# The adaLN modulation as column-tiled matmuls and the sums of squares run up on VectorE, in a fused block of linear attention, FFN, HGRN and Fourier mixing

## Chip, cores and metric

One core of one Trainium2 chip. The metric is the device time of one launch in microseconds (us), median of the runs. The engines are named PE (TensorE, the matrix engine), DVE (VectorE), ACT (ScalarE), POOL (GpSimd) and SP (SyncE, which here only starts DMA transfers). Everything is fp32. "Plain fp32" products appear in the trace as two LDWEIGHTS/MATMUL records each; the large linear layers use instead a split of each operand into a high part in the type fp32r and a low rest, and three products of one record each.

## What is computed

A token sequence of 512 (width 1024) goes through a hybrid layer (a gated delta rule with 4 heads beside a dilated attention with 8 heads, output projection, FFN of width 2816) and then through a second block of two layers: a gated recurrence (HGRN, 16 heads, with a context of 256 tokens) and a Fourier mixer. Two things in it matter here. Each layer of the second block scales, shifts and gates by a vector made from a conditioning vector `c` (and `c_ctx` for the context in the first layer):

```python
def rms_norm(x, g):
    var = jnp.mean(xf * xf, axis=-1, keepdims=True)
    return (xf * lax.rsqrt(var + EPS)).astype(x.dtype) * g

def adaln(cvec, w, b):
    m = jax.nn.silu(cvec) @ w + b          # (1024) @ (1024, 3072), two layers
    return jnp.split(m, 3, axis=-1)
...
        sh_l, sc_l, gt_l = adaln(c, ada_w[i], ada_b[i])
        h_lat = rms_norm(x_lat, norm_g[i]) * (1.0 + sc_l[:, None]) + sh_l[:, None]
...
        x_lat = x_lat + gt_l[:, None] * y_lat
```

And seven times the root mean square of a token's 1024 features is needed.

## The kernel before

The activations lie with features on the 128 partitions: 1024 features are KT = 8 blocks of a partition tile by 512 tokens. A linear layer is cut into units: a unit is a weight block of 1024 rows (8 blocks k) by 128 columns, 512 KB, loaded by SP (L361) into one of NST = 4 slots of `stage`, in the order of the list `units`. SP waits at each load until the slot is free (`stage_free`), and so a load that waits holds up every load behind it. ACT copies the slot to the high part `wh` (L975, `high`), DVE subtracts to the low part `wl` (L1362, `weight_low`, which frees the slot), both NSPLIT = 3 units ahead of PE. PE then runs 8 x 3 matmuls of 512 columns into one of three PSUM banks (L477 to L479). A tile is what one PSUM bank collects, one unit mostly, two units for `hg_w_out`.

**The modulation.** `ada_w` has 2 layers of 24 column blocks. Each is a further unit in the same list, not linear (`lin=False`, "raw" below). POOL (block at L414) multiplies the whole slot by the silu of the vector (L431, 128x1024), adds halves to 512 (L435) and to 256 columns (L439) in `mod`; PE sums over the partitions with two plain fp32 matmuls of one moving column (L460). The first 16 blocks of layer 0 are done for two vectors, so there are 40 such sums for layer 0 and 24 for layer 1. The 40 run during the attention and the delta rule, where PE takes them at the end of a step (`modulation(step)`, 32 steps, up to 1.3 sums a step). The other 24 stand in the FFN: two raws after each of the first two column pairs of a round, one after the later ones, until there are none left.

**The FFN.** Three rounds of 8, 8 and 6 column pairs. A pair is two `w_up` units (gate and up half); ACT evacuates each (L1183), DVE convolves (L1623, L1626), ACT applies silu (L1185), DVE multiplies (L1630), ACT and DVE split (L1187, L1632, semaphore `flo`). After the pairs the 8 tiles of `w_down` need all of them in order. In `finish_tile(t)` ACT first makes the high part of the unit three ahead and then waits for tile t, so evacuations stand behind that load in its queue.

**The norms.** After each tile n of a layer that adds to the residual, DVE adds the bank to `xT` (L1399 or L1401, `residual`), behind the low part of the weights three units ahead; ACT squares it to `sq` (L993, two buffers); PE adds over the partitions and over n with `ones` as stationary operand, a plain fp32 matmul of 512 columns (L512, `sum_mm`), 8 for each norm, placed one tile late. After the last `w_down` round there are two norms at once, of x and of x scaled by `final1`, 16 matmuls. The context norm (256 columns) runs in FFN round 2. The first norm, at the start, is not touched.

The attention stage in between has one more set of names: `g_*` are 128x512 tiles of the delta rule, `G["m.."]`, `xx`, `xt`, `tt` its doubling steps; `sm`, `pr`, `pT` are the attention's scores, probabilities and their transposes.

## Time and profile before

| | us |
|---|---|
| three runs | 2291.93, 2295.78, 2300.16 |
| median | 2295.78 |
| the profiled execution | 2289.31 |
| its span, first to last instruction | 2287.6 |
| busy in it: PE / DVE / ACT / POOL | 2125.4 / 1432.6 / 770.8 / 285.2 |
| mean granted TensorE clock | 0.964 |

The profiled execution is 6.5 us under the median and 1.7 us over its own span. Busy time is the union of an engine's instructions. The rows that later sections rest on are quoted in a section of their own; times in them are us from the start of the span unless marked ns.

### The profile page before, as it was taken

The page shows a single profiled execution, that of the slowest core. Times are in us where ns is not written, and L with a number is a line of the kernel's source. Part 1 is how long each engine was busy: PE and PEld are TensorE (multiplying, and loading weights), DVE is VectorE, ACT ScalarE, POOL GpSimd, SP SyncE. Part 2 cuts the span into 40 slices and gives each one's busy share as a digit, 9 for nine tenths or more (in the row PEclk, how much of TensorE's full clock was granted, in tenths as well). Part 3 has the DMA queues.
Part 4 walks back from the last instruction along what each step waited for, and adds up shares of the span by engine and source line. Part 5 has one row for each costly group of instructions (what it writes and reads, how often), then busy time and mean ns, then how long its engine had stood idle before and what let it go on. Part 6 is the DMA issues. An engine that isn't in the chain of part 4 may idle for free.

```text
span 2287.6 us, 27275 instructions
## 1 busy us (share of the span) xinstructions
PE 2125.4 (93%) x10891; PEld 1739.3 (76%) x10891; DVE 1432.6 (63%) x2240; ACT 770.8 (34%) x1145; POOL 285.2 (12%) x196
## 2 busy tenths in 40 slices
PE   6998778888999999799999999999999698999997
PEld 4876666656888887588888888888888586687875
DVE  5623777836847676568777887788877732433332
ACT  4363222244324433422333333323223323432222
POOL 0002677503413131000000000000000000000000
PEclk9999898888999999899999999999999799999999
DMA  4331111223434343111111111111111032132220
GB/s 143 100 85 39 45 47 47 74 89 103 140 102 138 111 118 113 55 56 48 55 56 47 56 47 56 47 56 47 47 56 54 12 109 66 39 91 83 83 83 37
DMA packets 311134, 164.58 MB, mean 72 GB/s; under 512 B 6268, under 2 KB 307938, under 8 KB 311010
## 3 DMA queue, kind: packets, MB, share of 16 engines
q1 hardware_dynamic: 311010, 162.85, 24.5%
q8 instruction: 87, 1.43, 0.3%
q14 instruction: 37, 0.30, 0.0%
HBM read 160.73 MB, written 2.10 MB: 71 GB/s over the span
## 4 chain that ended last, share of the span: by engine, by line
PE 75%; DVE 16%; issue 4%; ACT 4%; POOL 0%; SPq 0%; DMA 0%; DVEq 0%; ACTq 0%; POOLq 0%
PE bank L477 18%; PE bank L479 17%; PE bank L478 17%; PE bank L797 3%; DVE KC L1729 2%; DVE MT L1756 2%; DVE QQ L1735 2%; DVE QC L1731 2%; PE bank L512 2%; PE bank L496 1%; PE bank L495 1%; PE bank L494 1%; PE bank L913 1%; PE bank L841 1%; PE bank L822 1%
## 5 line engine op out<-in xcount | busy, mean ns | idle before, releaser
L1362 DVE TENSOR_TENSOR wl<-stage,wh 128x1024 fp32r<-128x1024 f32 (+1 forms) x248 | 310.6, 1254 | 581.7 <-ACT wh L975 581.6
L477 PE MATMUL bank<-hh,wh 128*128 128x512 f32 x1408 | 578.2, 411 | 31.8 <-DVE hl L1383 15.3
L975 ACT ACTIVATE wh<-stage 128x1024 fp32r<-128x1024 f32 (+1 forms) x248 | 260.0, 1050 | 924.3 <-PE bank L479 596.7
L479 PE MATMUL bank<-hh,wl 128*128 128x512 f32 x1408 | 553.8, 393 | 0.0
L478 PE MATMUL bank<-hl,wh 128*128 128x512 f32 x1408 | 552.6, 392 | 0.0
L477 PEld LDWEIGHTS bank<-hh,wh 128*128 128x128 f32 x1408 | 267.0, 190 | 92.7 <-issue 32.5
L479 PEld LDWEIGHTS bank<-hh,wl 128*128 128x128 f32 x1408 | 266.4, 189 | 58.3
L478 PEld LDWEIGHTS bank<-hl,wh 128*128 128x128 f32 x1408 | 267.7, 190 | 48.1 <-issue 0.7
L477 PE MATMUL bank<-gh,wh 128*128 128x512 f32 x432 | 180.0, 417 | 14.0 <-DVE gl L1888 5.1
L431 POOL TENSOR_TENSOR mprod<-stage,gs 128x1024 f32<-128x1024 f32 x64 | 131.2, 2050 | 462.3 <-DMA stage<-in_ada_w 457.5
L478 PE MATMUL bank<-gl,wh 128*128 128x512 f32 x432 | 170.3, 394 | 0.0
L479 PE MATMUL bank<-gh,wl 128*128 128x512 f32 x432 | 170.0, 394 | 0.0
L797 PEld LDWEIGHTS bank<-QC,KC 128*128 128x128 f32 x1024 | 132.1, 197 | 30.9 <-issue 27.3
L797 PE MATMUL bank<-QC,KC 128*128 128x128 f32 x1024 | 141.9, 283 | 14.4 <-DVE MT L1756 12.6
L477 PEld LDWEIGHTS bank<-gh,wh 128*128 128x128 f32 x432 | 82.4, 191 | 38.5 <-DVE gl L1888 6.5
L494 PE MATMUL bank<-ch,wh 128*128 128x256 f32 x384 | 111.0, 289 | 0.0
L495 PE MATMUL bank<-cl,wh 128*128 128x256 f32 x384 | 108.6, 283 | 0.0
L496 PE MATMUL bank<-ch,wl 128*128 128x256 f32 x384 | 108.6, 283 | 0.0
L435 POOL TENSOR_TENSOR mprod<-mprod 128x512 f32<-128x512 f32 x64 | 100.9, 1576 | 5.0
L478 PEld LDWEIGHTS bank<-gl,wh 128*128 128x128 f32 x432 | 82.5, 191 | 21.3 <-issue 4.8
L1729 DVE TENSOR_TENSOR KC<-KK,QQ 128x512 f32<-128x512 f32 x112 | 79.2, 707 | 29.0 <-PE bank L797 29.0
L479 PEld LDWEIGHTS bank<-gh,wl 128*128 128x128 f32 x432 | 82.2, 190 | 17.7
(307 smaller groups left out, 3149.0 us busy)
## 6 DMA issues: line engine op xcount, KB each, us to landing
stage<-in_hg_w_in SPq DMA_DIRECT2D x80, 512.0 KB, 3.6
stage<-in_ada_w SPq DMA_DIRECT2D x48, 512.0 KB, 3.6
stage<-in_w_up SPq DMA_DIRECT2D x44, 512.0 KB, 3.8
stage<-in_ft_w_in SPq DMA_DIRECT2D x32, 512.0 KB, 3.9
stage<-in_w_in SPq DMA_DIRECT2D x28, 512.0 KB, 3.8
stage<-in_w_down SPq DMA_DIRECT2D x16, 512.0 KB, 3.9
stage<-in_hg_w_out SPq DMA_DIRECT2D x16, 512.0 KB, 4.0
stage<-in_ft_w_out SPq DMA_DIRECT2D x16, 512.0 KB, 3.8
```

Source lines behind the costliest of these rows:

```text
L431: do(nc.gpsimd.tensor_tensor(mprod[:], stage[:, u["slot"], :, :], view(silc[:, v:v + 1], [[2, KT], [0, P]]), ALU.mult), f"stage_free{u['sl ...
L435: do(nc.gpsimd.tensor_tensor(mprod[:, 0:4, :], mprod[:, 0:4, :], mprod[:, 4:8, :], ALU.add))
L477: pe.matmul(bank[t % NLIN][:], wh[:, s, k, :], xh[:, k, :], start=a, stop=False)
L478: pe.matmul(bank[t % NLIN][:], wh[:, s, k, :], xl[:, k, :], start=False, stop=False)
L479: mm = pe.matmul(bank[t % NLIN][:], wl[:, s, k, :], xh[:, k, :], start=False, stop=b)
L494: pe.matmul(o, wh[:, s, k, :], ch[:, k, :], start=a, stop=False)
L495: pe.matmul(o, wh[:, s, k, :], cl[:, k, :], start=False, stop=False)
L496: mm = pe.matmul(o, wl[:, s, k, :], ch[:, k, :], start=False, stop=b)
L797: mm = pe.matmul(b[:, a * P:(a + 1) * P], kc[:, a * P:(a + 1) * P], qc[:, a * P:(a + 1) * P], start=True, stop=True)
L975: do(A.activation(wh[:, l % NSPLIT, 0:nk, :], stage[:, u["slot"], 0:nk, :], ACT.Copy), "hi_ready")
L1362: do(X.tensor_tensor(wl[:, l % NSPLIT, 0:nk, :], stage[:, u["slot"], 0:nk, :], wh[:, l % NSPLIT, 0:nk, :].bitcast(F32), ALU.subtract), f"s ...
L1729: do(X.tensor_tensor(view(kc[:, 0:1], flat), view(KK[:, 0, 0:1], sel), view(QQ[:, 0, 0:1], sel), ALU.mult))
```

## The change

**Modulation.** POOL does nothing any more. A raw unit is now 4 blocks of rows by 256 columns of `ada_w` (still 512 KB, in rows of 1 KB instead of 512 B), 48 of them, two (`kh` 0 and 1) to a block of 256 outputs, 12 blocks a layer. `silp` holds silu(c) and silu(c_ctx) in columns 0 and 1 of 32, the rest zero. PE itself waits for the slot and runs four plain fp32 matmuls per unit (L450 of the changed kernel): stationary `silp` 128x32, moving the 256 weight columns, the k-th one into partitions 32k to 32k+31 of bank 7, that is with the k-th column tile of the array. ACT copies the bank to `modrow` (`mod_rows`), and PE turns and adds the four partial rows with two matmuls against the 128x2 constant `pick` (`mod_columns`, L494). Layer 0 is done in 12 of the 33 attention steps, layer 1 between the two units of the first 12 FFN pairs. Both vectors are always computed. A raw's slot is now freed by PE, at PE's place in the program.

**Sums of squares.** For five of the norms (numbers m = 1, 2, 3, 5, 6), DVE adds squares 1 to 6 to their predecessors (`running`, L1446 and L1448), between the low part of the weights and the residual of the next tile, and PE runs two matmuls at the end (`sum_of`, four at the double norm) in place of eight (sixteen). ACT's square n waits for the running sum before it.

```diff
@@ -54,15 +54,14 @@
+BLOCKS = 12
+SQ_ADDS = {1: 0, 2: 6, 3: 12, 5: 24, 6: 30}
+SQ_SUMS = {1: 8, 2: 10, 3: 12, 5: 16, 6: 18}
...
@@ -112,8 +112,8 @@
-    raws = [dict(w="ada_w", layer=l, rows=(0, 8), col=j * P, lin=False, raw=l * 24 + j)
-            for l in range(2) for j in range(24)]
+    raws = [dict(w="ada_w", layer=l, rows=(4 * kh, 4), col=j * 2 * P, lin=False, raw=(l * BLOCKS + j) * 2 + kh)
+            for l in range(2) for j in range(BLOCKS) for kh in range(2)]
     late = raws[24:]
@@ -125,8 +125,9 @@
                 add("w_up", (0, 8), half * FF + j * P, "h")
-            units.extend(late[:2 if j < 2 else 1])
-            late = late[2 if j < 2 else 1:]
+                if half == 0:
+                    units.extend(late[:2])
+                    late = late[2:]
         for n in range(KT):
...
@@ -411,33 +424,6 @@
-        @block.gpsimd
...
-                        do(nc.gpsimd.tensor_tensor(mprod[:], stage[:, u["slot"], :, :], view(silc[:, v:v + 1], [[2, KT], [0, P]]),
-                                                   ALU.mult),
-                           f"stage_free{u['slot']}" if end else None, u["load"] + 1 if end else None)
-                        do(nc.gpsimd.tensor_tensor(mprod[:, 0:4, :], mprod[:, 0:4, :], mprod[:, 4:8, :], ALU.add))
-                            pool.wait_ge(S("mod_mm"), n - 1)
-                        do(nc.gpsimd.tensor_tensor(mod[:, n % 2, :, :], mprod[:, 0:2, :], mprod[:, 2:4, :], ALU.add), "mod_ready")
@@ -451,15 +437,19 @@
+                    j, kh = u["raw"] // 2, u["raw"] % 2
+                    if u["raw"] == 0:
+                        pe.wait_ge(S("silc_ready"), 2)
                     if u["raw"] == 24:
                         pe.wait_ge(S("ada0"), 1)
-                    for v in modulated(u["raw"]):
-                        n = modulation_sums(u["raw"]) + v
-                        pe.wait_ge(S("mod_ready"), n + 1)
-                        for k in range(2):
-                            mm = pe.matmul(bank[7][:, 2 * u["raw"] + v:2 * u["raw"] + v + 1], mod[:, n % 2, k, :],
-                                           ones[:, 0:1], start=(k == 0), stop=(k == 1))
-                        mm.then_inc(S("mod_mm"), 1)
+                    pe.wait_ge(S(f"stage_in{slot}"), 16 * (u["load"] + 1))
+                    if kh == 0 and j:
+                        pe.wait_ge(S("mod_ev"), j)
+                    w = raw_view(u)
+                    for k in range(4):
+                        mm = pe.matmul(bank[7][32 * k:32 * k + 32, 0:2 * P], silp[:, 4 * kh + k, :], w[:, k, :],
+                                       start=(kh == 0), stop=(kh == 1))
+                    mm.then_inc(S(f"stage_free{slot}"), 1)
                     return
@@ -496,6 +486,14 @@
+            def mod_columns(j):
+                pe.wait_ge(S("mod_ev"), j + 1)
+                for i in range(2):
+                    c = 2 * P + 2 * (2 * j + i)
+                    mm = pe.matmul(bank[7][:, c:c + 2], modrow[:, j % 2, i * P:(i + 1) * P], pick, start=True, stop=True)
+                mm.then_inc(S("mod_mm"), 1)
...
@@ -512,13 +510,14 @@
-            def residual_units(t0, sums, first_x):
-                for n in range(KT):
-                    units_to(t0 + n, first_x if n == 0 else None)
-                    if n:
-                        sums(n - 1)
-                sums(KT - 1)
+            def sum_of(m, part, width=T, b=3, buf=sq):
+                if part == 0:
+                    pe.wait_ge(S("sq_add"), SQ_ADDS[m] + (12 if m == 3 else 6))
+                else:
+                    pe.wait_ge(S("sq_ready"), KT * m + (2 * KT if m == 3 else KT))
+                pe.matmul(bank[b][:, 0:width], ones[:], buf[:, part, 0:width], start=(part == 0), stop=(part == 1)
+                          ).then_inc(S("sq_used"), 1)
@@ -612,10 +611,12 @@
-                while not units[pos[0]]["lin"] and modulation_sums(units[pos[0]]["raw"] + 1) <= 1.3 * (step + 1):
-                    unit(units[pos[0]])
-                    pos[0] += 1
+                if step - 1 in MOD_STEP:
+                    mod_columns(MOD_STEP[step - 1])
+                if step in MOD_STEP:
+                    for _ in range(2):
+                        unit(units[pos[0]])
+                        pos[0] += 1
...
@@ -743,19 +748,18 @@
                         mm.then_inc(S("cx_T"), 1)
-                        if j:
-                            sum_mm(2 * KT + j - 1, j - 1, CT)
                 if r < 2:
...
                     if r == 1:
-                        sum_mm(3 * KT - 1, KT - 1, CT)
+                        for part in range(2):
+                            sum_of(2, part, CT)
                     units_to(t1_ + KT - 1)
...
                         units_to(t1_ + n, ("flo", pairs) if n == 0 else None)
-                        for k in ([n - 1] if n else []) + ([n] if n == KT - 1 else []):
-                            sum_mm(3 * KT + 2 * k, k)
-                            sum_mm(3 * KT + 2 * k + 1, k, b=4)
+                    for part in range(2):
+                        sum_of(3, part)
+                        sum_of(3, part, b=4, buf=facc)
                 pairs += len(ROUND[r])
...
@@ -992,6 +999,19 @@
+            def square_of(m, n, src, name, value, width=T):
+                if n < 2:
+                    act.wait_ge(S("sq_used"), SQ_SUMS[m])
+                else:
+                    act.wait_ge(S("sq_add"), SQ_ADDS[m] + (2 if m == 3 else 1) * (n - 1))
+                act.wait_ge(S(name), value)
+                do(A.activation(sq[:, n % 2, 0:width], src, ACT.Square), "sq_ready")
+                if m == 3:
+                    if n == 0:
+                        act.wait_ge(S("flo"), FT)
+                    do(A.activation(facc[:, n % 2, :], src, ACT.Square, scale=vcol("final1", n)), "sq_ready")
...
@@ -1031,6 +1051,13 @@
+            def mod_rows(j):
+                u = raw_last[j]
+                act.wait_ge(S(f"stage_free{u['slot']}"), u["load"] + 1)
+                if j >= 2:
+                    act.wait_ge(S("mod_mm"), j - 1)
+                do(A.activation(modrow[:, j % 2, :], bank[7][:, 0:2 * P], ACT.Copy), "mod_ev")
...
@@ -1181,6 +1216,8 @@
                         evac(t, A.activation(fraw[:, 2 * (p % 2) + half, 2:2 + T], bank[t % NLIN][:], ACT.Copy))
+                    if p < BLOCKS:
+                        mod_rows(BLOCKS + p)
                     act.wait_ge(S("fconv"), 2 * p + 1)
...
@@ -1400,8 +1436,20 @@
+            def running(m, n, width=T):
+                if not 0 < n < KT - 1:
+                    return
+                dve.wait_ge(S("sq_ready"), KT * m + (2 * n + 2 if m == 3 else n + 1))
+                if n > 1:
+                    dve.wait_ge(S("sq_add"), SQ_ADDS[m] + (2 if m == 3 else 1) * (n - 1))
+                do(X.tensor_tensor(sq[:, n % 2, 0:width], sq[:, n % 2, 0:width], sq[:, (n - 1) % 2, 0:width], ALU.add), "sq_add")
+                if m == 3:
+                    do(X.tensor_tensor(facc[:, n % 2, :], facc[:, n % 2, :], facc[:, (n - 1) % 2, :], ALU.add), "sq_add")
...
             do(X.memset(halfeps, EPS), "const_set")
+            do(X.memset(silp[:], 0.0), "silp_zero")
             for k in range(KT):
...
@@ -1608,6 +1656,7 @@
                 weights_behind(T_OUT + n)
+                running(1, n - 1)
                 residual(T_OUT + n, n)
@@ -1631,8 +1680,12 @@
                     p += 1
+                    if r == 1:
+                        running(2, j - 1, CT)
                 for n in range(KT):
                     weights_behind(t1_ + n)
+                    if r == 2:
+                        running(3, n - 1)
                     residual(t1_ + n, n)
...
```

Order of PE's instructions in the attention stage, steps 2 and 3 of the first token block; `m_87` and `m_88` are the two level masks, L670 (L671 changed) the matmul that opens a step. Before:

```order
L588 MATMUL bank<-bqkv 128x384
L670 MATMUL bank<-g_xx,g_m_87 128x128 x4
L600 MATMUL bank<-ident,pr 128x128 x2
L680 MATMUL bank<-g_tt,g_xt 128x128 x4
L683 MATMUL bank<-g_xt,g_tt 128x128 x4
L588 MATMUL bank<-bqkv 128x512
L670 MATMUL bank<-g_xx,g_m_88 128x128 x4
L460 MATMUL bank<-ones,mod 128x1 x4
L600 MATMUL bank<-ident,pr 128x128 x3
```

and changed:

```order
L587 MATMUL bank<-bqkv 128x384
L671 MATMUL bank<-g_xx,g_m_87 128x128 x4
L450 MATMUL bank<-stage,silp 32x256 x8
L599 MATMUL bank<-ident,pr 128x128 x2
L681 MATMUL bank<-g_tt,g_xt 128x128 x4
L684 MATMUL bank<-g_xt,g_tt 128x128 x4
L587 MATMUL bank<-bqkv 128x512
L671 MATMUL bank<-g_xx,g_m_88 128x128 x4
L494 MATMUL bank<-small,modrow 128x2 x2
L599 MATMUL bank<-ident,pr 128x128 x3
```

The eight matmuls of a block stand where two small sums stood every other step, and the two that turn the rows a step later.

PE in the FFN between the two `w_up` units of a pair, where one raw stood. Before:

```order
L477 MATMUL bank<-hh,wh 128x512
L478 MATMUL bank<-hl,wh 128x512
L479 MATMUL bank<-hh,wl 128x512
L460 MATMUL bank<-ones,mod 128x1 x2
L477 MATMUL bank<-hh,wh 128x512
L478 MATMUL bank<-hl,wh 128x512
```

and changed (the L494 is that of the block before):

```order
L467 MATMUL bank<-hh,wh 128x512
L468 MATMUL bank<-hl,wh 128x512
L469 MATMUL bank<-hh,wl 128x512
L494 MATMUL bank<-small,modrow 128x2 x2
L450 MATMUL bank<-stage,silp 32x256 x8
L467 MATMUL bank<-hh,wh 128x512
L468 MATMUL bank<-hl,wh 128x512
```

The eight matmuls are now in the row of linear units, and so is PE's wait for the slot.

DVE in the tiles of `w_out` (L1362 and L1398 are the low part of the weights, L1399 and L1435 the residual). Before:

```order
L1362 TENSOR_TENSOR wl<-stage,wh 128x1024
L1399 TENSOR_TENSOR xT<-xT,bank 128x512
L1362 TENSOR_TENSOR wl<-stage,wh 128x1024
L1399 TENSOR_TENSOR xT<-xT,bank 128x512
L1362 TENSOR_TENSOR wl<-stage,wh 128x1024
L1399 TENSOR_TENSOR xT<-xT,bank 128x512
```

and changed:

```order
L1398 TENSOR_TENSOR wl<-stage,wh 128x1024
L1435 TENSOR_TENSOR xT<-xT,bank 128x512
L1398 TENSOR_TENSOR wl<-stage,wh 128x1024
L1446 TENSOR_TENSOR sq<-sq 128x512
L1435 TENSOR_TENSOR xT<-xT,bank 128x512
L1398 TENSOR_TENSOR wl<-stage,wh 128x1024
L1446 TENSOR_TENSOR sq<-sq 128x512
L1435 TENSOR_TENSOR xT<-xT,bank 128x512
```

From the third tile on an addition stands ahead of each residual.

## Rows read from the trace of the kernel before

**Rows 1.** Page of the kernel before, parts 1 and 2: busy time, granted clock

```profile
PE 2125.4 (93%) x10891; PEld 1739.3 (76%) x10891; DVE 1432.6 (63%) x2240; ACT 770.8 (34%) x1145; POOL 285.2 (12%) x196
...
PEclk9999898888999999899999999999999799999999
```

**Rows 2.** Busy time by stretch, two stretches, with its line of columns

```profile
core 0: us, PE busy (x) PEld busy (x) DVE busy (x) ACT busy (x) POOL busy (x), PEclk, DMA share, GB/s
207.00:460.00 253.00, 206.00 (x1240) 164.98 (x1240) 189.76 (x420) 62.84 (x127) 156.64 (x112) 0.88 0.17 49
552.00:625.00 73.00, 73.00 (x340) 60.85 (x339) 63.37 (x63) 27.35 (x38) 35.33 (x22) 1.00 0.46 137
```

**Rows 3.** Chain of waits by line, 207 to 460 us, shares of that stretch

```profile
by line: PE bank L609 9.2%; issue 8.1%; PE bank L683 6.2%; PE bank L670 5.8%; DVE pr L1488 5.3%; PE bank L680 4.6%; PE bank L588 4.1%; PE bank L460 3.5%; DVE g_tt L1512 2.8%; PE bank L633 2.7%; DVE pr L1493 2.5%; DVE g_ee L1525 2.5%; PE ban
```

**Rows 4.** Chain of waits by line, 230 to 245 us

```profile
by line: POOL mprod L431 15.9%; PE bank L680 11.9%; POOL mprod L435 11.5%; DVE pr L1493 11.2%; PE bank L683 10.4%; POOL mod L439 9.8%; PE bank L670 7.3%; PE bank L588 7.0%; PE bank L460 6.4%; PE bank L600 6.2%; issue 2.7%; POOLq L411 0.1%
```

**Rows 5.** Groups by line, DVE, 207 to 460 us: busy us, mean ns, idle

```profile
L1488 DVE CUSTOM_DVE_ANT_0 pr<-sm,dcnt 128x128 f32<-128x128 f32 (+3 forms) x32 | 24.9, 778 | 0.0
L1553 DVE TENSOR_TENSOR g_m<-g_lt,gmask 128x512 f32<-128x512 f32 x20 | 24.3, 1213 | 0.0
L1493 DVE TENSOR_SCALAR pr<-pr,gs 128x128 f32<-128x128 f32 (+3 forms) x32 | 23.7, 739 | 1.1
L1512 DVE TENSOR_SCALAR g_tt<-cst,gs 128x128 f32<-128x128 f32 x16 | 8.2, 575 | 10.7 <-ACT gs L1102 10.7
```

**Rows 6.** Single lines on DVE: duration ns min/median/max, first and last start

```profile
L1553 DVE TENSOR_TENSOR g_m<-g_lt,gmask x20: 682/1157/2202, 223.8 to 439.0; 128x512 f32<-128x512 f32 x20
L1488 DVE CUSTOM_DVE_ANT_0 pr<-sm,dcnt x32: 277/678/1917, 222.1 to 452.9; 128x128 f32<-128x128 f32 x8, 128x256 f32<-128x256 f32 x8, 128x384 f32<-128x384 f32 x8, 128x512 f32<-128x512 f32 x8
L1493 DVE TENSOR_SCALAR pr<-pr,gs x32: 286/562/1672, 222.7 to 453.8; 128x128 f32<-128x128 f32 x8, 128x256 f32<-128x256 f32 x8, 128x384 f32<-128x384 f32 x8, 128x512 f32<-128x512 f32 x8
L1512 DVE TENSOR_SCALAR g_tt<-cst,gs x16: 272/280/1918, 208.8 to 396.2; 128x128 f32<-128x128 f32 x16
```

**Rows 7.** Timeline at 294 and 454 us: start us, us, engine, line

```profile
293.83 0.95 PE L460 MATMUL bank<-ones,mod 128*128 128x1 f32 x8
294.89 1.06 PE L680 MATMUL bank<-g_tt,g_xt 128*128 128x128 f32 x8
...
453.81 0.48 DVE L1493 TENSOR_SCALAR pr<-pr,gs 128x512 f32<-128x512 f32 x1
```

**Rows 8.** Timeline, w_out and last w_down: start us, us, engine, line

```profile
490.51 1.02 PE L512 MATMUL bank<-sq,ones 128*128 128x512 f32 x2
496.85 1.02 PE L512 MATMUL bank<-sq,ones 128*128 128x512 f32 x2
...
931.71 1.88 PE L512 MATMUL bank<-sq,ones 128*128 128x512 f32 x4
...
938.91 1.22 DVE L1362 TENSOR_TENSOR wl<-stage,wh 128x1024 fp32r<-128x1024 f32 x1 [4.02 <-ACT wh L975]
940.05 0.68 DVE L1399 TENSOR_TENSOR xT<-xT,bank 128x512 f32<-128x512 f32 x1
```

**Rows 9.** Timeline: fp32 products of 64 stationary columns, of 256 moving columns

```profile
311.04 2.37 PE L609 MATMUL bank<-pT,bqkv 128*64 128x512 f32 x8
...
715.92 0.60 PE L512 MATMUL bank<-sq,ones 128*128 128x256 f32 x2
716.35 0.50 PE L460 MATMUL bank<-ones,mod 128*128 128x1 f32 x4
```

**Rows 10.** Chain of waits, 552 to 625 us: start us, us, what

```profile
578.76 0.34 PE bank L460 x4
590.15 0.34 PE bank L460 x4
```

**Rows 11.** DMA, 550 to 640 us, and the page's row of these loads

```profile
GB/s 0 147 316 3 64 343 66 0 167 303 228 4 0 53 337 309 0 11 61 345 289 5 0 84 348 267 0 0 88 345 263 10 0 107 317 274 1 156 77 62
...
stage<-in_ada_w SPq DMA_DIRECT2D x48, 512.0 KB, 3.6
```

More of the change, by code:

```diff
@@ L205, in build @@
         raw = at("raw", A0 + 56, [P, 2, T + 8])
-        mprod = at("mprod", A0 + 56, [P, KT, P])
-        mod = at("mod", A0 + 60.25, [P, 2, 2, P])
+        modrow = at("modrow", A0 + 60.25, [P, 2, 2 * P])
+        silp = at("silp", A0 + 73, [P, KT, 32])
         cst = at("cst", A0 + 62.25, [P, 2 * P])
@@ L282, in build @@
         halfeps = small[:, 0:1]
-        onecol = small[:, 1:32]
+        pick = small[:, 1:3]
         ada = small[:, 32:128]
@@ L304, in build @@
         T_OUT, T_UP, T_HG, T_HO, T_FT = FIRST["w_out"], FIRST["w_up"], FIRST["hg_w_in"], FIRST["hg_w_out"], FIRST["ft_w_in"]
+        MOD_STEP = {2 + (8 * j) // 3: j for j in range(BLOCKS)}
+        raw_last = {u["raw"] // 2: u for u in units if not u["lin"]}
         ffn_tiles = []
@@ L730, in _ @@
                 units_to(T_OUT + n)
-                sum_mm(KT + n - 1, n - 1)
-            sum_mm(2 * KT - 1, KT - 1)
+            for part in range(2):
+                sum_of(1, part)
             pairs = 0
@@ L735, in _ @@
                 for j in range(len(ROUND[r])):
-                    units_to(t0 + 2 * j + 1, ("h_ready", KT) if r == 0 and j == 0 else None)
+                    units_to(t0 + 2 * j, ("h_ready", KT) if r == 0 and j == 0 else None)
+                    if 1 <= pairs + j <= BLOCKS:
+                        mod_columns(BLOCKS + pairs + j - 1)
+                    units_to(t0 + 2 * j + 1)
                     if r == 1:
@@ L755, in _ @@
                         units_to(t1_ + n, ("flo", pairs) if n == 0 else None)
-                        for k in ([n - 1] if n else []) + ([n] if n == KT - 1 else []):
-                            sum_mm(3 * KT + 2 * k, k)
-                            sum_mm(3 * KT + 2 * k + 1, k, b=4)
+                    for part in range(2):
+                        sum_of(3, part)
+                        sum_of(3, part, b=4, buf=facc)
                 pairs += len(ROUND[r])
@@ L896, in _ @@
                 if n:
-                    sum_mm(5 * KT + n - 1, n - 1)
                     turn_x(n - 1)
-            sum_mm(6 * KT - 1, KT - 1)
+            for part in range(2):
+                sum_of(5, part)
             turn_x(KT - 1)
@@ L945, in _ @@
                     else:
-                        residual_units(t + 4, lambda k: sum_mm(6 * KT + k, k), mixed_in)
+                        units_to(t + 4, mixed_in)
+                        units_to(t + 4 + KT - 1)
+                        for part in range(2):
+                            sum_of(6, part)
             assert pos[0] == len(units)
@@ L1336, in _ @@
                         finish_tile(t + 4 + n)
-            residual_tiles(len(tiles) - KT, 6 * KT)
-            root(rs, bank[3], value=7 * KT)
+            residual_tiles(len(tiles) - KT, 6)
+            root(rs, bank[3], value=SQ_SUMS[6] + 2)
             for i in range(2 * TT):
```

85 lines of the change are left out of this document (40 added, 45 removed).

## The prediction

> **What bounds the kernel now.** I read the page first, then busy time by stretch, the chain of waits in two stages, the groups on DVE and the timeline at the places that the change touches. PE is busy 93% of the span at a clock near full, POOL only 12% [rows 1]. By stretch there are two kinds of stage. In the linear layers PE is never idle (73.00 of 73.00 us in the first FFN round, clock 1.00), while DVE has 63.37 of 73 and ACT 27.35 [rows 2]: what PE sheds there is won in full and what it gets is paid in full. In the attention stage, 207 to 460 us, PE is busy 206.0 of 253 us, DVE 189.8, POOL 156.6, at a clock of 0.88 [rows 2]. Its chain goes back and forth between PE and DVE, with the small sums L460 on it for 3.5% of 253 = 8.9 us [rows 3]; twice PE waits for POOL itself, once in 230 to 245 us, where POOL's three lines are 15.9 + 11.5 + 9.8 = 37.2% of 15 us = 5.6 us [rows 4], and once like it near 305 us, together 11 us.
>
> **Sums of squares.** A tile of `w_out` comes every 496.85 - 490.51 = 6.34 us [rows 8]. An FFN pair of two equal units and one L460 sum comes every 590.15 - 578.76 = 11.39 us [rows 10]; with 0.50 for the sum [rows 9] a unit is 5.44. So a sum of squares costs PE 0.90. Eight become two. The seventh (k = 6) and the eighth stood behind the last tile, in the time in which PE waits for the last residual, and so do the two that are left; what is won is six: 5.4 us at each of norms 1, 5 and 6, 16.2 together. The context norm: six of 0.43 (715.92 to 716.35 for 256 columns [rows 9]) = 2.6. The double norm: two sums a tile take 1.88, with what overlaps the next about 1.8 [rows 8], times 6 = 10.7. Sum -29.5. DVE gets 30 additions of 512 columns and 6 of 256. An addition of two SBUF tiles of 512 takes 0.68 at the least (L1553 [rows 6]), 23 us in all. They lie beside PE's next unit, where DVE stood idle 4.02 us a tile [rows 8]. They cost at one place: behind the last tile DVE first makes the low part of weights to come (938.91), then the residual (940.05) [rows 8], and the addition of square 6 now stands between, since it follows the low part in the queue. That is 0.68 at norms 1 and 5, 1.36 at the double one, nothing at norm 6, where no weights follow: +2.7. Net **-27**. Without DVE's cover (if residual n came over 5 us late) each addition would cost 0.7, 23 us; nothing near that is in the rows.
>
> **POOL leaves, attention stage.** The same DVE instruction takes 682 to 2202 ns at L1553 and 272 to 1918 at L1512 [rows 6], means 1213 and 575 [rows 5]. The long ones coincide with POOL's. I take the excess over the short ones: L1553 20 x 0.53 = 10.6; L1512 16 x 0.295 = 4.7; L1488 has four widths from 277 ns [rows 6] to about 0.68, mean 0.48, against 778: 32 x 0.30 = 9.5; L1493 from 286 to 0.48 at full width [rows 7], mean 0.385, against 739: 32 x 0.354 = 11.3 [rows 5]. That is 36 us of DVE, not all on the chain: L1488 has 5.3% of 253 = 13.4 of its 24.9 us there, L1493 6.3 of 23.7, L1512 7.1 of 8.2 [rows 3, 5]. By these shares 5.1 + 3.0 + 4.1, and for L1553, of which that row shows no share, a quarter, 2.7: 15. With POOL's own 11 that is 26. What is late next is PE's own row of small matmuls, so I keep three quarters: **-20**. Bounds: 0 if PE is next at once, -36 - 11 = -47 if DVE were all of the chain.
>
> **PE's new work.** No row shows column tiles side by side. A plain fp32 product of 256 columns is two records, together 0.43, thus 0.215 a record [rows 9]. A block is 8 products, 16 records. One after the other: 16 x 0.215 = 3.44. All four tiles at once: 2 x 0.43 = 0.86. Between them: records run in order, and a product's second record needs the same column tile as its first, so only the second of one and the first of the next can overlap; 16 records take 9 places, 1.94. I take this one, by the order in which records of a product stand in pairs; it is an argument, and both ends stay in the range. Changing the tile shape: L609 (64 columns stationary, 1280 columns moved) took 2.37 [rows 9] where 5 x 0.43 = 2.15 is moving time, so at most 0.2 for both changes; I add 0.12 a block. So a block is 2.06, and `mod_columns`, four records like L460, 0.50 more [rows 9].
>
> A rule of the Trainium skill speaks for the faster end: the page "TensorE: Matmul & The Clock Gate", section "Part 3: Packing small matmuls", says that matmuls in different column groups run at the same time, and gives 2.38x for three of them. By it a block would be near the 0.86, which is the second case below; that the products here are pairs of records it doesn't treat. Against it stands the page "TensorEngine Tiling (Array Packing)", section "Key Properties": changing the tiling mode drains the engine. The L609 row leaves at most 0.2 us for it.
>
> *FFN.* Out: 24 sums of 0.50 = 12.0. In: 12 x (2.06 + 0.50) = 30.7. PE is full there, so **+19**.
>
> *Attention.* Before, a sum step's L460 (0.95 at 293.83) fits between the step's matmul and L680 at 294.89, which needs ACT's copy anyway [rows 7]. 40 sums go; half of their 8.9 us on the chain counts, -4. The first 0.95 of a block fits into the same gap, the rest, 1.1, is added at 12 steps: +13. `mod_columns` fits into the gap of its own step. ACT's 24 copies of 256 columns lie in its idle time (62.84 busy of 253 [rows 2]). Together **+9**.
>
> *End of an FFN round.* ACT's evacuation of a gate tile now stands behind a load that waits for PE's raw. At the end of round 1 the split products for `w_down` come later by what that load waits, less what DVE gains from POOL's leaving: **+1**.
>
> **Sum:** -27 - 20 + 19 + 9 + 1 = -18 us against the profiled execution (2289.3), so 2271 for such a one; it lay 6.5 under the median of three, and against that median of 2295.8 the same -18 gives **2277**.
>
> **The rivals.**
>
> 1. *All tiles at once.* A block is 0.98. FFN 12 x 1.48 - 12.0 = +6; attention -20 - 4 + 0. Sum -27 + 6 - 24 + 1 = -44: 2252. For it: that nothing in the rows forbids it; against: the pairs.
> 2. *No overlap, the other side.* A block is 3.44 + 0.12 = 3.56. FFN 12 x 4.06 - 12.0 = +37; attention -20 - 4 + 12 x 2.6 = +7. Sum -27 + 37 + 7 + 1 = +18: 2314. For it: the products of L609, all in one column half, run one behind the other at full price [rows 9]; against: they had to, being one tile. Break-even is a block of about 2.8 us.
> 3. *The loads.* SP's queue is in order, so the next pair's `w_up` loads stand behind raws that wait for PE. After a block three loads of 0.52 MB at 345 GB/s take 4.6 us behind a first landing of 3.6 [rows 11], and the two halves of the split need some 2.4 more (1.22 for DVE [rows 8], the same for ACT as an estimate): 10.6 us, and the unit is due 2 x 5.44 + 0.5 = 11.4 us later. There is under 1 us to spare. If transfers queue worse, each of 11 pairs waits 1 to 3 us: +11 to +33, near 2297.
> 4. *A higher clock.* 0.88 means that a quarter of the 253 us ran at 1.2 GHz instead of 2.4. If PE's idle stretches go with POOL, up to 15 us come on top of any case (half of 61 us, half of it PE's). I count it in the low end.
> 5. *Nothing from POOL's leaving* (PE is next at once): 2277 + 20 = 2297.
>
> **How the numbers follow.** Chances: the forecast 0.40, all at once 0.25, none 0.17, loads 0.08, nothing from POOL 0.10. The range 2242 to 2306 holds the first two with the clock above them, the loads and the last, and leaves out the case without overlap and a little at both ends, 0.2 in all. A measurement of this kernel can tell about 0.3% from no change, 7 us: under 2289 lie nearly all of the forecast and of rival 1, 0.66; within, parts of the forecast, of 3 and of 5, 0.13; above, rival 2 and the bad ends of 3 and 5, 0.21.
>
> **What the profile after would show.** Starts of the four stationary-`silp` products: in pairs 0.43 apart (rival 2), 0.2 apart per record place (forecast), or nearly together (rival 1). The FFN pair period: 11.39 less 0.50 plus 2.56 = 13.45 as forecast, 12.4 or 14.9 in the rivals, 14.5 and more with PE waiting for `stage` in rival 3. `w_out` tiles every 5.44, the last `w_down` tiles every 4.1. L1553 and L1512 all at 0.68 and 0.28. The attention stage about 11 us shorter than 253. The prediction is wrong if a block isn't 1.9 to 2.2 us, or if DVE's gain doesn't shorten the stage.

## The result, and the profile after

The changed kernel took 2257.72 us (median of 4 runs, 2253.23 to 2259.41), the kernel before 2297.97 beside it: ratio 0.9826, 95% interval 0.9800 to 0.9851. The profiled execution (2253.23, span 2251.5) ends 36.1 us of span earlier than that of before, where the sum said 18: twice the gain. Page, parts 1 and 2:

```profile
PE 2095.2 (93%) x11043; PEld 1708.3 (76%) x11043; DVE 1363.3 (61%) x2277; ACT 776.9 (35%) x1169; POOL 0.2 (0%) x4
...
PEclk9999899989999999799999999999999799999998
```

DVE, with 37 more instructions, is busy 69 us less [rows 1]. Busy time by stretch, the attention stage and most of the first FFN round:

```profile
core 0: us, PE busy (x) PEld busy (x) DVE busy (x) ACT busy (x) POOL busy (x), PEclk, DMA share, GB/s
207.00:430.00 223.00, 193.89 (x1320) 145.51 (x1320) 151.53 (x420) 66.18 (x141) 0.00 (x0) 0.92 0.18 56
526.00:600.00 74.00, 72.64 (x396) 57.10 (x397) 43.02 (x58) 26.25 (x39) 0.00 (x0) 1.00 0.55 171
```

The same 420 DVE instructions take 151.53 us where they took 189.76 [rows 2]. The lines of [rows 5], in the same order with the changed kernel's numbers, and L1609 (L1561 before: 24 times, 683 ns), which reads PSUM:

```profile
L1536 DVE CUSTOM_DVE_ANT_0 pr<-sm,dcnt 128x128 f32<-128x128 f32 (+3 forms) x32 | 15.5, 484 | 0.0
L1601 DVE TENSOR_TENSOR g_m<-g_lt,gmask 128x512 f32<-128x512 f32 x20 | 13.6, 682 | 0.0
L1541 DVE TENSOR_SCALAR pr<-pr,gs 128x128 f32<-128x128 f32 (+3 forms) x32 | 12.4, 386 | 1.1
L1560 DVE TENSOR_SCALAR g_tt<-cst,gs 128x128 f32<-128x128 f32 x16 | 3.5, 279 | 10.7 <-ACT gs L1130 10.7
...
L1609 DVE TENSOR_TENSOR g_xt<-g_xt,bank 128x512 f32<-128x512 f32 x24 | 16.5, 688 | 8.0 <-PE bank L684 7.6
```

A block in the FFN, timeline of PE:

```profile
564.51 0.50 PE L494 MATMUL bank<-small,modrow 128*128 128x2 f32 x4
564.95 1.07 PE L450 MATMUL bank<-stage,silp 128*32 128x256 f32 x16
```

The 16 records of a block took 1.07 us. And the last `w_down`, one tile and the start of the next, ACT and DVE:

```profile
884.91 0.83 ACT L982 ACTIVATE wh<-stage 128x768 fp32r<-128x768 f32 x1
...
885.77 0.96 DVE L1398 TENSOR_TENSOR wl<-stage,wh 128x768 fp32r<-128x768 f32 x1 [2.13 <-ACT wh L982]
886.65 0.68 DVE L1446 TENSOR_TENSOR sq<-sq 128x512 f32<-128x512 f32 x1
887.25 0.69 DVE L1448 TENSOR_TENSOR facc<-facc 128x512 f32<-128x512 f32 x1
887.85 0.68 DVE L1435 TENSOR_TENSOR xT<-xT,bank 128x512 f32<-128x512 f32 x1
...
888.65 0.63 ACT L1009 ACTIVATE sq<-xT 128x512 f32<-128x512 f32 x1 [2.91 <-DVE xT L1435]
889.19 0.71 ACT L1013 ACTIVATE facc<-xT,V 128x512 f32<-128x512 f32 x1
889.80 0.83 ACT L982 ACTIVATE wh<-stage 128x768 fp32r<-128x768 f32 x1
...
890.66 0.96 DVE L1398 TENSOR_TENSOR wl<-stage,wh 128x768 fp32r<-128x768 f32 x1 [2.13 <-ACT wh L982]
```

A tile comes every 4.89 us; the last three, beside which weights of 1024 rows are split and not of 768, come every 5.37. Each stretch in the changed kernel minus that before gives a table of where the time went. The last column is the same kernel, profiled once more as `g_again`: two executions of one program differ by up to 2.4 us in a stretch, and no entry can be read closer than that.

| Stretch | Measured | The sum had | Profiled again |
|---|---|---|---|
| attention stage (ends 460.24, now 429.34) | -30.9 | -11 (-20 + 9) | -30.0 |
| `w_out` with norm 1 | -5.2 | -4.7 | -3.3 |
| FFN to the last `w_down`, context norm among it | +10.5 | +17.4 (19 + 1 - 2.6) | +12.1 |
| last `w_down` and double norm | -3.0 | -9.3 | -0.7 |
| HGRN | +0.8 | 0 | +1.1 |
| norms 5 and 6 | -8.4 | -10.1 | -10.8 |
| all | -36.1 | -18 | -31.6 |

Of the 2.3 us between the two executions at the double norm, the granted clock is the visible difference: in `g_again` it is at its lower level from 876.6 to 880.0 us, behind PE's wait of 2.75 us, as it is in the kernel before (896.9 to 900.3), and in the changed kernel's own profile it stays at the higher level there.

### The profile page after: what moved, and what is told of

Its sections match the earlier page's. It is cut to its first block, busy times and chain, and to the rows that moved or that the text cites. A ratio compares the mean times of both kernels' runs of the same rounds, so it can differ in the third digit from the quotient of the medians.

```text
span 2251.5 us, 27398 instructions
## 1 busy us (share of the span) xinstructions
PE 2095.2 (93%) x11043; PEld 1708.3 (76%) x11043; DVE 1363.3 (61%) x2277; ACT 776.9 (35%) x1169; POOL 0.2 (0%) x4
## 4 chain that ended last, share of the span: by engine, by line
PE 75%; DVE 15%; ACT 4%; issue 4%; DMA 1%; SPq 0%; DVEq 0%; ACTq 0%
PE bank L467 17%; PE bank L469 17%; PE bank L468 17%; PE bank L801 3%; DVE KC L1782 2%; DVE MT L1809 2%; DVE QQ L1788 2%; DVE QC L1784 2%; PE bank L486 1%; PE bank L485 1%; PE bank L484 1%; PE bank L671 1%; PE bank L917 1%; PE bank L845 1%; PE bank L826 1%
## 5 line engine op out<-in xcount | busy, mean ns | idle before, releaser
L1398 DVE TENSOR_TENSOR wl<-stage,wh 128x1024 fp32r<-128x1024 f32 (+1 forms) x248 | 301.1, 1215 | 608.8 <-ACT wh L982 608.8
L467 PE MATMUL bank<-gh,wh 128*128 128x512 f32 x432 | 171.9, 398 | 17.2 <-DVE gl L1681 7.4
L468 PEld LDWEIGHTS bank<-gl,wh 128*128 128x128 f32 x432 | 82.3, 191 | 17.4 <-issue 0.5
L1809 DVE COPY_PREDICATED MT<-hmask,bank 128x512 f32<-128x512 uint32 x128 | 94.3, 736 | 0.0
L1784 DVE TENSOR_TENSOR QC<-qs,PP 128x512 f32<-128x512 f32 x112 | 79.0, 706 | 0.0
```

The source lines that it names most:

```text
L467: pe.matmul(bank[t % NLIN][:], wh[:, s, k, :], xh[:, k, :], start=a, stop=False)
L468: pe.matmul(bank[t % NLIN][:], wh[:, s, k, :], xl[:, k, :], start=False, stop=False)
L1398: do(X.tensor_tensor(wl[:, l % NSPLIT, 0:nk, :], stage[:, u["slot"], 0:nk, :], wh[:, l % NSPLIT, 0:nk, :].bitcast(F32), ALU.subtract), f"s ...
L1784: do(X.tensor_tensor(view(qc[:, 0:1], flat), view(q[:, 0:1], flat), view(PP[:, 0, 0:1], [[2 * n, nb], [n - T, 2], [1, n]], T), ALU.mult), ...
L1809: do(X.copy_predicated(MT[:], view(hmask[:, li, :], [[0, 4], [1, P]]), bank[4 + li % 2][:].rearrange("p (a c) -> p a c", c=P)), "lv_ev%d" ...
```

## The experiments

The theory has three parts: a block runs all four column tiles at once; the attention stage got shorter because DVE is no longer held up by GpSimd; at the double norm a loop of ACT and DVE sets the pace. The rivals are that the block is cheap for another reason, and that the attention stage gained from PE's waits for GpSimd, from the small sums that went, or from a higher clock.

### The two halves of the change

`a_mod` is the changed kernel with the eight matmuls a norm of the kernel before (an excerpt of the edit):

```diff
-            for part in range(2):
-                sum_of(5, part)
+                    sum_mm(5 * KT + n - 1, n - 1)
+            sum_mm(6 * KT - 1, KT - 1)
```

> The changed kernel with the sums of squares put back as eight (sixteen) matmuls on PE: the modulation alone. The changed kernel is some 40 us under the one before. My theory, from the two traces: the sums are worth 5.4 at w_out, 3 at the double norm, 8.4 at the two norms of the HGRN and about 1.5 at the context norm, 18 in all, so this kernel lies 18 above the changed one, at about 2276, 22 under the kernel before; its attention stage (207 to 429 us) is as short as in the changed kernel and its last w_down tiles come every 7.1 us as before. Rival (the prediction's own size of the sums, 27, with some 9 lost to a cause outside the sums): about 2285.

Measured 2274.87 us, ratio to before 0.9917 (0.9901 to 0.9934), 19 under the kernel before. The attention stage ends at 431.88, 2.5 us behind the changed kernel's. The theory had 2276 and holds, the rival's 2285 does not. The text's 7.1 us for the last `w_down` tiles is a misreading: they come every 5.85 us here, as in the kernel before.

`b_sums` is the kernel before with the additions on DVE (`running`) and the two matmuls at the end (`sum_of`) alone.

> The kernel before with the running sums of squares alone; the modulation stays on GpSimd. My theory: 18 us under the kernel before, about 2280; the last w_down tiles come every 4.9 us or more, held by the loop ACT, DVE, ACT, and not every 4.1; L1553 still varies from 0.68 to 2.2 us. If the two parts add up, its gain and that of the modulation alone make the 40 us. Rival: GpSimd takes part of the gain because DVE, which now has 36 more instructions, is slowed by it in the FFN: under 14 us gained, and the double norm no shorter than before.

Measured 2280.63, ratio 0.9945 (0.9928 to 0.9961), 13.6 under it, where the theory had 18 and the rival under 14. The halves give 19 + 14 = 33 of the 38 to 40. Up to the second round's `w_down` its trace is 3.6 us ahead, and after it 3.4 behind: PE waits 5.31 us for `gl` there (0.74 before). In each pair of this round ACT's square of the context waits for the addition, which stands in DVE's row behind `gl`, and ACT's next high part stands behind that square:

```profile
772.52 0.69 DVE L1663 TENSOR_TENSOR gl<-facc,gh 128x512 fp32r<-128x512 f32 x1 [0.70 <-ACT gh L1207]
773.13 0.42 DVE L1429 TENSOR_TENSOR sq<-sq 128x256 f32<-128x256 f32 x1
...
773.59 0.42 ACT L1009 ACTIVATE sq<-craw 128x256 f32<-128x256 f32 x1 [0.82 <-DVE sq L1429]
773.91 1.04 ACT L982 ACTIVATE wh<-stage 128x1024 fp32r<-128x1024 f32 x1
```

The rival's cause is in it too. While GpSimd works, up to 762 us, ACT's high parts of the products (`gh`) come up to 12.69 us apart where PE takes 11.6 a pair, so ACT and DVE fall behind; when it has stopped, they come 10.27 apart (9.53 before, where the square waits for nothing), and that does not catch up. In the changed kernel, with the same square and addition but without GpSimd, the wait at that place is 1.62.

### What a block costs

`d_onetile` puts the same eight products into one column tile:

```diff
-                        mm = pe.matmul(bank[7][32 * k:32 * k + 32, 0:2 * P], silp[:, 4 * kh + k, :], w[:, k, :],
-                                       start=(kh == 0), stop=(kh == 1))
+                        mm = pe.matmul(bank[7][0:32, 0:2 * P], silp[:, 4 * kh + k, :], w[:, k, :],
+                                       start=(kh == 0 and k == 0), stop=(kh == 1 and k == 3))
```

> The changed kernel with the eight products of a block all in the first column tile (partitions 0 to 31 of the bank, added up by PSUM); the rows and their turning then read 32 partitions instead of 128. It computes the same. Theory: in four column tiles all run at once, and in one tile they run one behind the other: a block of 16 records goes from 1.07 us to about 3.5, 2.4 more; 12 times in the FFN, where PE is full, is 29 us, and of the 12 in the attention stage half or more shows, 12 to 29: 2299 to 2316. Rival: a block costs what its records cost to issue, whatever the tile; then it stays near 1.1 us and the time near 2258.

Measured 2315.72 us, ratio 1.0094 (1.0079 to 1.0109), slower than the kernel before. The block's row:

```profile
558.41 3.64 PE L450 MATMUL bank<-stage,silp 128*32 128x256 f32 x16
```

It took 3.64 us against 1.07. The attention stage ends 29.8 us later, and the rest adds 30.8: 24 times 2.57 is 61.7, the whole span is 60.5 longer.

`f_quarter` runs one tile of four from the second block on and leaves out the other three quarters of each sum:

```diff
-                    for k in range(4):
+                    for k in (range(4) if u["raw"] < 2 else range(1)):
```

> The changed kernel, which from the second block on runs only the first of the four column tiles: 2 of a block's 8 products. The other three quarters of each sum are left out. Theory: the four tiles run at once, so a block goes from about 1.0 us to about 0.9, and 23 blocks to 1 to 3 us less in all. Rival: the products queue up and a block is only cheap for another reason; then a quarter of the products takes a quarter of the time, 0.7 to 0.8 less a block, and 15 us go.

Measured 2256.03, ratio 0.9825 (0.9806 to 0.9844), against 2259.30 and 0.9843 (0.9826 to 0.9861) for the changed kernel beside it. The row:

```profile
539.23 1.05 PE L450 MATMUL bank<-stage,silp 128*32 128x256 f32 x4
```

Four records in one tile take 1.05 us, sixteen in four tiles take 1.07: three tiles of four are free, and so the pairs of records of an fp32 product do overlap across tiles. The 15 us of the rival are not there, 3.3 are.

> The changed kernel once more, unedited, on the chip on which the two below run: some 38 to 40 us under the kernel before, and the level from which they are read.

It was 36 us under.

### Where the attention stage's 31 us went

`c_pool` lets GpSimd work beside the changed kernel, without use for its results (40 times; the excerpt shows the product, the two additions are as before):

```diff
+                do(nc.gpsimd.tensor_tensor(big, view(xT[:, 0, 0:1], [[T, KT], [1, P]]), view(silp[:, 0, n % 2:n % 2 + 1], [[32, KT], [0, P]]),
+                                           ALU.mult))
```

> The changed kernel, with GpSimd doing beside it, in the attention stage, the same 40 times three instructions as in the kernel before (product of 1024, sums of 512 and 256 columns), on tiles of its own. Nothing waits for it but one instruction of ACT at the end of the delta rule; its results are not used. The loads, the small sums and the rest of PE stay as in the changed kernel. Theory A: of the 31 us that the attention stage lost, most came from DVE being held up by GpSimd; then the stage grows by 15 to 25 us here, L1553 varies up to 2 us again, and the time is 2273 to 2283. Theory B: they came from PE no longer waiting for GpSimd and from the 40 small sums leaving the chain; then DVE is slower but the stage grows by less than 8 us, and the time is at most 2266.

Measured 2277.47, ratio 0.9931 (0.9909 to 0.9952). The stage ends at 455.25 us, 25.9 later. Its stretch, and the masks' line, single instructions:

```profile
207.00:456.00 249.00, 203.47 (x1334) 153.42 (x1332) 189.37 (x421) 67.26 (x141) 152.17 (x108) 0.90 0.16 51
...
L1621 DVE TENSOR_TENSOR g_m<-g_lt,gmask x20: 680/1061/2431, 227.3 to 433.6; 128x512 f32<-128x512 f32 x20
```

DVE is back at 189 us with the same instructions, and the list of waits shows no engine waiting for GpSimd. So GpSimd costs the stage its time by holding up DVE, as theory A has it.

`e_small` puts the 40 small sums back into the changed kernel's PE row:

```diff
+                    for k in range(2):
+                        pe.matmul(bank[7][:, 500:501], ident[:], ones[:, 0:1], start=(k == 0), stop=(k == 1))
```

> The changed kernel, with 40 small sums (two plain fp32 matmuls of one moving column each, into unused columns of the same bank) put back in PE's row in the attention stage, at the steps where the kernel before had them. They wait for nobody, and their results are not used. Theory: the prediction priced their going at 4 us, half of their 8.9 on the chain; the attention stage grows by 4 to 9 us. Rival: the gaps of a step swallow them, under 2 us, and what the stage gained beyond GpSimd's slowing of DVE is all from PE no longer waiting for GpSimd.

Measured 2275.23, ratio 0.9909 (0.9891 to 0.9927). The stage ends at 448.94, 18.7 later than in `g_again` (430.21): both theory and rival missed. The row of the small sums, 207 to 449 us:

```profile
L617 PE MATMUL bank<-ones,ident 128*128 128x1 f32 x160 | 23.6, 267 | 0.0
```

Of 23.6 us of busy time 18.7 show: with DVE no longer held up, PE's own row is the path.

`h_light` is the kernel before with little work for GpSimd (29 us busy in the stage where it was 157); most of the modulation vector is left out:

```diff
+                        c = P if n < 2 else 1
-                        do(nc.gpsimd.tensor_tensor(mprod[:], stage[:, u["slot"], :, :], view(silc[:, v:v + 1], [[2, KT], [0, P]]),
+                        do(nc.gpsimd.tensor_tensor(mprod[:, :, 0:c], stage[:, u["slot"], :, 0:c], view(silc[:, v:v + 1], [[2, KT], [0, c]]),
```

> The kernel before, in which GpSimd from the third vector on makes its products and its sums for one of 128 columns only (8, 4 and 2 elements a partition), in the attention stage and in the FFN; the rest of the modulation vector is left out. PE's 40 small sums stay where they are, and no blocks are there. Theory: the attention stage loses what GpSimd cost it, 22 us by holding up DVE (as it grew when GpSimd was put back) and the 2.4 us in which PE waited for GpSimd: it ends 25 us earlier, the FFN changes by under 2 us, the time is about 2270. Against the changed kernel with the small sums put back, whose stage ended 21.8 us before that of the kernel before, the difference is what 12 blocks with their turning cost there: at full price 12 x 1.57 = 19 us, by which the stage here would end 40 us earlier and not 25. The two can't both hold; my money is on the first, with the blocks costing little because ends don't add up. Rival: with DVE no longer held up the stage stands by PE's own row, and blocks cost in full: 36 to 40 us earlier, 2255 to 2259.

One figure in that text is wrong: the stage with the small sums ended 460.24 - 448.94 = 11.3 before that of the kernel before, not 21.8, so blocks at full price would have meant 30 us here and not 40. Measured 2266.97, ratio 0.9874 (0.9855 to 0.9893), 29 under by medians and 22.4 by the spans of the profiled executions. The stage ends at 436.24, 24.0 earlier, and the trace stays 23.1 ahead through the whole FFN. Its stretch:

```profile
207.00:437.00 230.00, 199.51 (x1240) 158.43 (x1240) 151.51 (x421) 62.35 (x129) 29.48 (x112) 0.89 0.18 53
```

This orders the account. From before to here GpSimd's work leaves: -24.0. From here to `e_small` (small sums in both) the blocks come: 448.94 - 436.24 = +12.7. From there to the changed kernel the small sums leave: -18.7. Together that is -30.0, which it has to be, since each step starts where the last one ended; the 0.9 to the 30.9 of the table is the difference between two executions of the changed kernel. Another order of the steps could divide the 30.0 otherwise, and none was run.

A part of every step is the clock. It was at its lower level for 61.4 us of the stage before, 51.2 in `h_light`, 44.4 in `e_small`, 47.8 in `c_pool`, and for 30.7 and 34.1 in the two profiles of the changed kernel. Linear matmuls take twice as long in such a stretch (0.43 against 0.23 us in `v4_spread`, below). If all of PE's work did, half of each difference would be the clock's: as an estimate some 5 us of the 24.0, 7 of the 18.7 (7 of `c_pool`'s 25.9 as well), and 14 of the whole 30.9. Most of each step is not the clock, but no run tells the two apart. `b_sums`, whose attention stage is that of the kernel before, shows how far it moves by itself: 68.3 us at the lower level, and an end 3.3 us later.

### The loop at the double norm, and a faster version

`v2_early` moves the additions ahead of the weights, at norms 1, 3, 5 and 6:

```diff
-                    weights_behind(t1_ + n)
                     if r == 2:
                         running(3, n - 1)
+                    weights_behind(t1_ + n)
```

> The changed kernel, with the running additions of the norms 1, 3, 5 and 6 ahead of the low part of the next weights in DVE's row instead of behind it. Theory: in the last w_down the tile period of 4.9 us is a loop: ACT's high part (0.83), DVE's low part (0.96), its two additions (1.38), ACT's two squares (1.34), and DVE's residual between; with the additions first the squares no longer wait for the weights, the loop opens, and the tiles come at PE's pace of about 4.1: 7 x 0.8 = 5 to 6 us less, and another 0.7 at each of the ends of norms 1 and 5: 2250 to 2252, 6 to 7 under the changed kernel. Rival: the period is held by the split of the weights (four slots, three tiles ahead) and not by the squares: the tiles stay at 4.9, nothing gained.

Measured 2244.56, ratio to before 0.9783 (0.9770 to 0.9796), below the changed kernel's interval, the fastest of all, and more than the 6 to 7 us that were expected: its span is 9.3 shorter than that of the changed kernel. The same place:

```profile
881.27 0.95 DVE L1398 TENSOR_TENSOR wl<-stage,wh 128x768 fp32r<-128x768 f32 x1
882.14 0.68 DVE L1435 TENSOR_TENSOR xT<-xT,bank 128x512 f32<-128x512 f32 x1
884.22 0.69 DVE L1446 TENSOR_TENSOR sq<-sq 128x512 f32<-128x512 f32 x1 [1.40 <-ACT facc L1013]
884.83 0.69 DVE L1448 TENSOR_TENSOR facc<-facc 128x512 f32<-128x512 f32 x1
885.43 0.95 DVE L1398 TENSOR_TENSOR wl<-stage,wh 128x768 fp32r<-128x768 f32 x1
```

Tiles come every 4.16 us instead of 4.89. From the first matmul of the last `w_down` to the first behind the double norm 54.30 us pass (61.05 in the changed kernel), 6.75 less. With the 3.0 of the table that is 9.7, some 2 of it the clock's, where the prediction had 9.3: its price of the sums was about right, and the loop had eaten it. Of the 9.3 by which the whole span is shorter, 1.4 came where norms 5 and 6 end; another 1.5 came in the first tile of `hg_w_out`, which differs as much between the two profiles of the changed kernel, and isn't put down to the edit.

`v3_rows` moves `mod_rows` to stand behind the gate tile's evacuation.

> As v2_early, and in the FFN ACT copies a block's four rows right behind its evacuation of the gate tile, not after the second tile. Theory: PE's waits for modrow, 1.7 us in the first FFN rounds of the changed kernel (0.33, 0.81 and 0.54 are the longest), go: 1 to 2 us under v2_early. Rival: ACT waits there for the raw's matmuls with the weights' high parts queued behind it, and the next unit comes late: 2 to 5 us over v2_early.

Measured 2247.83, 0.9796 (0.9783 to 0.9810): 3 over `v2_early` with intervals that overlap. PE no longer waits for `modrow`, but in `v2_early` it waited 0.3 us only, so there was nothing to win, and 1.7 of the difference arose in the attention stage, which has no edit. Neither theory is shown.

`v4_spread` changes one line of the planner:

```diff
-                if half == 0:
-                    units.extend(late[:2])
-                    late = late[2:]
+                units.extend(late[:1])
+                late = late[1:]
```

> As v2_early, with one raw behind each of the two w_up units of a pair instead of two behind the gate unit. Same work on every engine; only the order of the loads and of the halves of a block changes. Theory: the stall at the start of w_down (3.0 us in the first round, 1.6 in the second, against 1.4 and 0.7 before) comes from ACT and DVE waiting for weights behind two raws that PE frees late; spread, it falls to about what it was: 2 to 3 us under v2_early. Rival: it comes from the longer row of work on ACT and DVE itself and stays, within 1 us of v2_early.

Measured 2277.03, 0.9922 (0.9909 to 0.9936): 32 slower than `v2_early`, where at most 3 either way was expected. The chain of waits in one FFN pair:

```profile
565.97 0.61 PE bank L449 x8
...
566.60 0.37 SPq L369
567.01 5.28 DMA stage<-in_w_up
...
573.27 0.58 ACT fraw L1217
573.86 0.28 ACT modrow L1059
...
574.18 0.61 PE bank L493 x4
574.79 0.57 PE bank L449 x8
575.36 0.45 PE bank L466
```

The waits form a ring. PE's half block frees a slot, a `w_up` load of 5.28 us fills it, ACT makes its high part, and behind that in ACT's row stand the evacuation and `modrow`, for which PE waits (us, times, longest, in 495 to 960 us):

```profile
PE bank L493 <- ACT modrow L1059: 14.6, 10, 2.0
```

The blocks come every 14 to 17 us. In the changed kernel both halves stand together and ACT's copy lies ahead of such a load: they come every 12.45 at best. The last `w_down` starts 26.6 us later than in `v2_early`: 14.6 are these waits, and from 515 to 860 us the clock is at its lower level for 20.5 us, with PE busy, where `v2_early` has none, as an estimate another 10. The stall at `w_down`'s start shrank from 2.98 to 2.73 only, so the rival was right on that.

## Why the prediction was right, and where it was not

The direction held, and the time lies in the range, 20 us under the forecast (2295.8 - 18 is 2278, not 2277). But the gain was twice the 18 us, and by its own sign the prediction was wrong: a block is not 1.9 to 2.2 us. That the number held is in part luck, since large errors of opposite sign met: the attention stage and the block price came out better than their terms, the double norm and the waits in the FFN worse.

**Sums of squares, -27.** The price of a sum and the tail were right: norm 1 gave 5.2, or 3.3 profiled again (4.7 with its addition in the tail). `a_mod` puts all sums at 2274.87 - 2259.30 by medians, 15.6, or 21 by the two ratios (0.9917 - 0.9826); the table at 16.6, and 19.2 with the forecast's own 2.6 for the context norm. The term that failed is the double norm, -3.0 (or -0.7) for -9.3. The step was "they lie beside PE's next unit, where DVE stood idle 4.02 us a tile". The idle time was there, but the additions entered a loop: from start to start the high part takes 0.86, the low part 0.88, the additions 1.20, the residual 0.80, the squares 1.15, together 4.89 us, and then the next high part; PE would have needed 4.1. `v2_early` opens it and gets 6.75 us back.

**POOL leaving, -20.** 24.0 by `h_light`, 25.9 by `c_pool`. The excess of 36 us read from the four lines is 38 by the whole of DVE (189.76 - 151.53). The 11 us for "PE waits for POOL itself" were misread: a share of POOL's lines on the chain is POOL's work behind a wait, not the wait. The list of waits of the kernel before, 207 to 460 us (us, times, longest):

```profile
PE bank L460 <- POOL mod L439: 2.4, 2, 1.5
```

So DVE's excess weighed more than the 15 that its shares gave: some 22 (24.0 less 2.4, the clock's part included) of the 38 us were on the path. The term's -20 lies near the 24.0 because its 11 for POOL made up for that: luck, and not the reading.

**Attention, blocks and sums, +9.** The blocks measured +12.7 where +13 was forecast, which is chance: two thirds of 12 x (1.07 + 0.50) show, and not half of 12 x 2.06. The small sums were priced -4, half of their chain share, and gave 18.7, the clock's part included. This is the largest mis-sized term. Chain shares were read while DVE was slow and covered PE's small work; once DVE is quick, each instruction of PE counts. `d_onetile` says the same: 2.57 more a block gave 2.48 a block.

**Block price, 1.94 + 0.12.** Wrong: rival 1's 0.98 for 1.07. The argument from pairs ("only the second of one and the first of the next can overlap") fell with the 1.07 us, and `f_quarter` shows that the other tiles' records cost nothing beside the first tile's. The 2.38x for three column groups that the prediction took from the Trainium skill, "TensorE: Matmul & The Clock Gate", "Part 3: Packing small matmuls", bears out here with more: four groups of pairs in 1.07 where one tile takes 3.64, 3.4x.

**FFN, +19.** A pair with a block takes 12.45 at its shortest (552.46 to 564.95 is 12.49), rival 1's 12.4, so 12 x 1.56 - 12.0 = +6.7. The stretch lost 10.5, or 13.1 without the context norm's 2.6. The rest is waits: `modrow` 1.7 us (2.7 profiled again), and `w_down` starts that wait longer for `gl` (3.02 and 1.62 against 1.36 and 0.74, so 2.5 for the +1); some 2 us more stay unassigned. Rival 3 was near: ACT waits for a `w_up` load in every pair of the first round, seven times and 2.8 us at the least, and `v4_spread` shows what that costs when the last slack goes.

**A higher clock.** The stage had 0.92 for 0.88: it went the expected way. No run holds the clock still; by the estimate above some 14 of the 30.9 us are its own, near the 15 that rival 4 allowed.

So the time is that of rival 1 (-44) with some 14 us lost again, 6 at the double norm, 6 in the FFN and 2 at norms 5 and 6, and some 7 more gained in attention. The chances had this case at 0.25, the forecast at 0.40.

## What to carry over

A long chain share of a helper engine is its work behind a wait; read the wait itself in the list of waits. Where two engines take turns on the path, price each one's work as it will be when the other is quick: here the small matmuls that a slow DVE had covered cost 80% of their busy time afterwards. Before putting work into an idle gap, follow who waits for it: idle time inside a loop of two engines isn't free, and swapping two instructions' order won back what the loop had taken.

## What the runs showed of the hardware

- Four column tiles of 32 run at once, for plain fp32 as well: 16 records of 256 columns in 1.07 us, 4 in 1.05, and 3.64 for 16 in one tile. The two switches of tile shape, in and out, cost at most 0.2 us together: 1.07 against the 0.86 of one tile's two products (0.43 each [rows 9]).
- GpSimd's work slows some DVE instructions only. Those with two SBUF inputs (L1553: mean 1213 against 682 ns) and some with one (L1493, L1512) are held up, those with a PSUM input not (L1561: 683 and 688). They wait until GpSimd's instruction is over: 13 of the 20 at L1553 took longer than 0.69 us, and each of the 13 ended 0.55 us after the end of a GpSimd instruction that was under way when it started. The other way round GpSimd waits: a product that starts just behind L1553 takes up to 2.4 us instead of 1.90. In the kernel before:

```profile
237.17 0.68 DVE L1553 TENSOR_TENSOR g_m<-g_lt,gmask 128x512 f32<-128x512 f32 x1
237.24 2.38 POOL L431 TENSOR_TENSOR mprod<-stage,gs 128x1024 f32<-128x1024 f32 x1
...
359.51 1.90 POOL L431 TENSOR_TENSOR mprod<-stage,gs 128x1024 f32<-128x1024 f32 x1
359.75 2.20 DVE L1553 TENSOR_TENSOR g_m<-g_lt,gmask 128x512 f32<-128x512 f32 x1
```

  The Trainium skill, page "SBUF — State Buffer", section "SBUF: two separate sides", calls the shared port an exclusive lock for a whole instruction; the trace agrees.
- After the 1.97 us in which PE waited in `v4_spread`, the next linear matmuls came 0.43 us apart, eight times, then 0.23 again (granted clock 0.72 over 574 to 580 us): the lower of the two levels, 1.2 GHz, follows such a gap, and about doubles its price. The length of the wait alone does not decide it: after 1.27 us at 604 the clock fell too (0.57 over 606 to 610 us), and after 1.42 us at 620 it did not (1.00 over 621 to 626).
